# Key and query preparation of a sparse-attention mixer spread over other work, the first norm tile by tile, and banks opened one at a time

## The reference

```python
def rms_norm(x, g):
    return x * rsqrt(mean(x * x, -1) + EPS) * g
def apply_rope_2(x, cos, sin):
    x1, x2 = split(x, 2, axis=-1)
    return concatenate([x1 * cos - x2 * sin, x2 * cos + x1 * sin], -1)

# first block: the norm that starts the kernel, then one projection
hn = rms_norm(h, mix_norm_pre[l]);  proj = hn @ w_in[l]
# each feed-forward layer: up products, gate, down products
y = (silu(a) * b) @ w_out

# third mixer: h is the modulated norm, 4 key heads, 16 query heads of 64
kv = h @ w_kv                                # k_cmp v_cmp k_sel v_sel k_win v_win
kc = rms_norm(silu(blocks(k_cmp) @ w1[0]) @ w2[0], k_norm[0])    # 31 compressed keys
vc = silu(blocks(v_cmp) @ w1[1]) @ w2[1]
ks = apply_rope_2(rms_norm(k_sel, k_norm[1]), cos, sin)
kw = apply_rope_2(rms_norm(k_win, k_norm[2]), cos, sin)
q  = rms_norm(h @ w_q, q_norm)
q_rope = apply_rope_2(q, cos, sin)
s_c = q @ kc * scale        # compressed branch uses q; the two others use q_rope
```

## Time and profile before

| | us |
|---|---|
| median of 3 runs (2306.75 to 2307.64) | 2307.42 |
| the execution that was profiled | 2307.61 |
| its span in the trace | 2305.8 |
| PE busy | 2135.4 (93%) |
| DVE busy | 1261.0 (55%) |
| ACT busy | 808.6 (35%) |
| POOL busy | 91.8 (4%) |

### The profile page before, as it was taken

One profiled execution on the slowest core, in us unless ns is written; L12 is line 12 of the kernel. 1 busy time (PEld: TensorE's weight loads), 2 busy tenths in 40 slices (PEclk: granted clock), 3 DMA queues, 4 the chain that ended last, 5 costly groups with the idle time before them and its releaser, 6 DMA issues.

```text
span 2305.8 us, 28424 instructions
## 1 busy us (share of the span) xinstructions
PE 2135.4 (93%) x10880; PEld 1738.8 (75%) x10880; DVE 1261.0 (55%) x2209; ACT 808.6 (35%) x1467; POOL 91.8 (4%) x88
## 2 busy tenths in 40 slices
PE   4998898999899899999999999999669999999998
PEld 3876576888788688887788877779546667888787
DVE  2578447777654423683755545664566756322234
ACT  3333445333323435213422222333236644222232
POOL 0002300000000010000000000000210110000000
PEclk8999899999999899999999999999779999999999
DMA  4321113556442132101465636323300013422221
GB/s 150 110 73 55 37 56 119 183 183 190 139 162 94 65 95 98 46 1 56 134 204 168 197 117 211 119 64 95 103 1 2 2 38 117 137 94 92 92 92 55
DMA packets 146642, 233.10 MB, mean 101 GB/s; under 512 B 7276, under 2 KB 83532, under 8 KB 146252
## 3 DMA queue, kind: packets, MB, share of 16 engines
q1 hardware_dynamic: 142304, 222.28, 29.9%
q10 hardware_dynamic: 3340, 5.85, 0.7%
q0 software_dynamic: 864, 3.15, 0.4%
HBM read 229.16 MB, written 2.10 MB: 100 GB/s over the span
## 4 chain that ended last, share of the span: by engine, by line
PE 78%; DVE 12%; ACT 4%; issue 4%; POOL 1%; DMA 0%; ACTq 0%; DVEq 0%; POOLq 0%
PE ps L2096 10%; PE ps L2098 10%; PE ps L2097 10%; PE ps L2121 4%; PE ps L2363 4%; PE ps L2122 4%; PE ps L2123 4%; PE ps L2280 4%; PE ps L2056 4%; PE ps L2058 4%; PE ps L2057 4%; PE ps L2282 3%; PE ps L2142 3%; PE ps L2154 2%; PE ps L2167 2%
## 5 line engine op out<-in xcount | busy, mean ns | idle before, releaser
L1512 DVE TENSOR_TENSOR w_lo<-ring,w_hi 128x1024 fp32r<-128x1024 f32 (+4 forms) x362 | 376.5, 1041 | 795.9 <-ACT w_hi L946 795.2
L946 ACT ACTIVATE w_hi<-ring 128x1024 fp32r<-128x1024 f32 (+4 forms) x362 | 329.5, 912 | 992.3 <-PE ps L2098 467.3
L2096 PE MATMUL ps<-x_hi,w_hi 128*128 128x512 f32 x1056 | 415.9, 394 | 0.0
L2098 PE MATMUL ps<-x_hi,w_lo 128*128 128x512 f32 x1056 | 411.2, 389 | 0.0
L2097 PE MATMUL ps<-x_lo,w_hi 128*128 128x512 f32 x1056 | 410.8, 389 | 0.0
L2097 PEld LDWEIGHTS ps<-x_lo,w_hi 128*128 128x128 f32 x1056 | 198.3, 188 | 42.7 <-issue 1.9
L2096 PEld LDWEIGHTS ps<-x_hi,w_hi 128*128 128x128 f32 x1056 | 198.3, 188 | 42.3 <-issue 1.9
L2098 PEld LDWEIGHTS ps<-x_hi,w_lo 128*128 128x128 f32 x1056 | 198.2, 188 | 41.7
L2121 PE MATMUL ps<-w_hi,x_hi 128*128 128x512 f32 x480 | 187.5, 391 | 3.7 <-DVE x_hi L1586 3.7
L2123 PE MATMUL ps<-w_hi,x_hi 128*128 128x512 f32 x480 | 186.8, 389 | 0.0
L2122 PE MATMUL ps<-w_lo,x_hi 128*128 128x512 f32 x480 | 186.8, 389 | 0.0
(11 more groups left out here) (308 smaller groups left out, 3148.8 us busy)
## 6 DMA issues: line engine op xcount, KB each, us to landing
ring<-in_ada_w SPq DMA_DIRECT2D x48, 1024.0 KB, 5.2
ring<-in_ffn_w_in SPq DMA_DIRECT2D x88, 512.0 KB, 4.6
ring<-in_w_up SPq DMA_DIRECT2D x44, 512.0 KB, 4.4
ring<-in_ffn_w_out SPq DMA_DIRECT2D x20, 1024.0 KB, 4.9
ring<-in_hgrn_w_in SPq DMA_DIRECT2D x16, 1024.0 KB, 5.1
ring<-in_w_in SPq DMA_DIRECT2D x12, 1024.0 KB, 5.0
ring<-in_w_down SPq DMA_DIRECT2D x10, 1024.0 KB, 4.9
ring<-in_kv_ada_w SPq DMA_DIRECT2D x8, 1024.0 KB, 5.1
```

What stands on the lines that cost most here:

```text
L946: a.activation(to[:, n % depth, 0:src.shape[-1]], src, ACT.Copy).then_inc(s["hi_done"], 1)
L1512: v.tensor_tensor(to[:, n % depth, 0:width], src, hi[:, n % depth, 0:width].bitcast(F32), ALU.subtract).then_inc(s["lo_done"], 1)
L2096: mm(bs[j], wh[:, k, c], x_hi[:, 2 * q + k], start=first, stop=False)
L2098: ins = mm(bs[j], wl[:, k, c], x_hi[:, 2 * q + k], start=False, stop=last)
```

## The change

**Start.** Only the identity and six row loads stay on ACT's queue. SP loads `x` in four tiles with a semaphore each and waits for nothing, then the unit `iq`, then all other constants (`load_constants`), then the rest of the weights. ACT loads its root table first and takes `x` tile by tile; the rounded parts of the first two weight pieces are made ahead of the norm's output (`EARLY[0]`). The normalized `x` lies where it no longer overlaps `x0_lo`, so DVE splits a bank as soon as it is there. The other rows are transposed into a bank `vec2` between the third and fourth piece of `iq`.

**Feed-forward.** PE opens each of the eight down banks right before its first product. DVE does `ada_out` before `up_gated`.

**Third mixer.** POOL multiplies the norm weights into rotation tables (`rope_g`) once, beside the projections, and is out of the chunks. The key chunks (four of 128x512) are normalized and rotated on DVE between pieces of `nq`. The eight query chunks stand among the products of the compressed keys, by the list `PREP`; the plain form is transposed without the norm weight, which `cmp_norm` now carries. `Q_CHUNKS` and `GROUPS` run from the last token tile to the first.

```diff
+EARLY[0] = [(("iq", q), "iq", q * PIECE, PIECE) for q in range(2)]
+Q_CHUNKS = [(t, j) for t in reversed(range(NT)) for j in range(2)]
+PREP = [("cmp1", 0, 0), ("q", 0), ("cmp1", 0, 1), ("q", 1), ("cmp1", 1, 0), ("q", 2), ("cmp1", 1, 1), ("q", 3), ("cmp2",),
+        ("q", 4), ("q", 5), ("cmpT",), ("q", 6), ("q", 7)]
-XN = {0: xn, ...
+XN = {0: y1, ...
...
 @block.sync
-    sp.wait_ge(s["x_in"], 16)
+    for t in range(NT):
+        sp.dma_start(x_tok[:, t], io["x"][0, t * P:(t + 1) * P, :]).then_inc(s[f"x_in{t}"], 16)
     for n, (pieces, _) in enumerate(units):
+        if n == 1:
+            load_constants()
...
 @block.gpsimd
+    evacuated(pool, ("kvs", 1, NT - 1))
+    pool.wait_ge(s["consts_in"], 32)
+    pool.wait_ge(s["cmp_pos_in"], 64)
+    for j in range(3):
+        gain = qk_norm[:, j, :].rearrange("p (q d) -> p q d", q=2)
+        cos, sin, nsin = [rope_t[:, i] for i in range(3)]
+        for q in range(2):
+            g.tensor_tensor(rope_g[:, j, :, 32 * q:32 * q + 32], cos, gain[:, q:q + 1].broadcast_to(...), ALU.mult)
+        g.tensor_tensor(rope_g[:, j, :, 64:96], nsin, gain[:, 1:2].broadcast_to(...), ALU.mult)
+        g.tensor_tensor(rope_g[:, j, :, 96:128], sin, gain[:, 0:1].broadcast_to(...), ALU.mult)
+    g.tensor_tensor(cmp_norm[:, :], cmp_norm[:, :], qk_norm[:, 0, :], ALU.mult).then_inc(s["tables_done"], 1)
-    for t in range(NT):
-        for j in range(3):
-            pool.wait_ge(s["raw_norm"], i + 1)
-            g.tensor_tensor(w, w, qk_norm[...].broadcast_to(...), ALU.mult).then_inc(s["gained"], 1)
...
 @block.scalar
+    act.dma_start(small[:, 0:P], io["c_small"][:, 0:P]).then_inc(s["ident_in"], 16)
-    act.dma_start(small[:, :], io["c_small"]).then_inc(s["consts_in"], 16)
-    act.dma_start(x_tok[:, :, :], ...).then_inc(s["x_in"], 16)
...
 def norm(i):
     if i == 0:
-        act.wait_ge(s["x_in"], 16)
         for t in range(NT):
+            act.wait_ge(s[f"x_in{t}"], 16)
             x_rms(0, t)
+        early_highs(0, slice(0, 2))
+        evacuated(act, "vec")
...
+    if (key, k) == (("nq", 0), 6):
+        raw_root(NT, slice(16, 24))
...
 @block.vector
-    if i == 0:
-        filled(dve, ("xT", 0, KT - 1))
     for kt in range(KT):
+        if i == 0 and kt in (0, 2):
+            early_lows(0, slice(kt // 2, kt // 2 + 1))
...
-    up_gated(i, FFN_UNITS - 1)
     for u in (FFN_UNITS - 2, FFN_UNITS - 1):
         for mj in ada_after.get((i, u), []):
             ada_out(*mj)
+    up_gated(i, FFN_UNITS - 1)
...
+    if (k, q) == (0, 3):
+        p = filled(dve, "vec2")
+        v.tensor_copy(vec[:, CONV:416], p[:, CONV:416]).then_inc(free("vec2"), 1)
+        step(v.tensor_copy(masks[:, :, :], mask_rows))
...
+def k_chunk(t):
+    a, b = n_a[:, t % 2], n_b[:, t % 2]
+    step(v.tensor_tensor(a, raw[:, t, 16:24, :], <reciprocals>, ALU.mult))
+    dve.wait_ge(s["tables_done"], 13)
+    for j in range(2):
+        rope_gained(a[:, f], t, 1 + j, b[:, f], ko[:, t, f], 4)
+    v.tensor_tensor(ko[:, t], b, ko[:, t], ALU.add).then_inc(s["rope2_done"], 1)
+K_CHUNK_AT = {(("nq", 0), 7): 0, (("nq", 1), 1): 1, (("nq", 1), 7): 2, (("nq", 2), 1): 3}
...
+def q_chunk(i):
+    dve.wait_ge(s["raw_norm"], 2 * i + 2)
+    if i >= 2:
+        filled(dve, ("nT", i - 2, 1))
+    rope_gained(n_a[:, i % 2], t, 0, n_b[:, i % 2], n_o[:, i % 2], 8)
+    if i + 1 < len(Q_CHUNKS):
+        q_norm(i + 1)          # waits for the plain transposes of chunk i - 1
+    v.tensor_tensor(n_o[:, i % 2], n_b[:, i % 2], n_o[:, i % 2], ALU.add).then_inc(s["rope2_done"], 1)
+for i in range(len(Q_CHUNKS)):
+    q_chunk(i)                 # then cmp_sums() after 4, cmp_keys() after 5, cmp_turned() after 6
...
 @block.tensor
-    bs = [open_bank(("down", i, j)) for j in range(8)]
+    bs = [None] * 8
...
+        if k == 0:
+            bs[2 * t + half] = open_bank(("down", i, 2 * t + half))
...
+    if (k, q) == (0, 2):
+        other_rows()
```

More of the change, by code:

```diff
@@ L866, in early_highs @@
                 for key, slot, at, n in EARLY.get(i, [])[some]:
[L867 removed]
+                    high(key, arrived(act, slot, (0,))[:, at:at + n], w2_hi if i in (2, 4) else w_hi if i else w0_hi)
             def post(stage):
@@ L1219, in n_result, with raw_root @@
                 ins.then_inc(free((name, u, k)), 1)
+            def raw_root(done, heads):
+                act.wait_ge(s["raw_done"], done)
+                sums, roots = [stat[:, at:at + 96].rearrange("p (t h) -> p t h", t=NT)[:, :, heads] for at in (32, 128)]
+                a.activation(roots, sums, ACT.Sqrt, scale=1.0 / HD, bias=eps[:, :]).then_inc(s["raw_rms"], 1)
             for g, (key, k) in enumerate(N_PIECES):
@@ L1288, in early_lows @@
                 for key, slot, at, n in EARLY.get(i, [])[some]:
-                    low(key, arrived(dve, slot, (0,))[:, at:at + n], *((w2_lo, w2_hi) if i in (2, 4) else (w_lo, w_hi)))
+                    low(key, arrived(dve, slot, (0,))[:, at:at + n], *((w2_lo, w2_hi) if i in (2, 4) else (w_lo, w_hi) if i else (w0_lo, w0_hi)))
             def norm(i):
@@ new lines, in cmp_sums @@
+            def cmp_sums():
+                p = filled(dve, "cmp2")
+                step(v.tensor_copy(kc_raw, p[0:NCMP, 0:256]))
+                v.memset(kc_t[:, :, :, :], 0.0).then_inc(s["cmp_zero"], 1)
+                dve.wait_ge(s["cmp_zero"], 2)
+                for gg in range(GROUP):
+                    ins = v.tensor_copy(vc_diag[32 * gg:32 * gg + NCMP, :, gg], p[0:NCMP, 256:512].rearrange("p (h d) -> p h d", h=4))
+                    if gg < GROUP - 1:
+                        step(ins)
+                ins.then_inc(free("cmp2"), 1)
+                after()
+                step(v.tensor_tensor(kc_tok, kc_raw.rearrange("p (h d) -> p h d", h=4), kc_raw.rearrange("p (h d) -> p h d", h=4), ALU.mult))
+                after()
+                v.tensor_reduce(stat[0:NCMP, 244:248], kc_tok, AX, ALU.add).then_inc(s["cmp_sq"], 1)
@@ new lines, in cmp_second @@
+            def cmp_second():
+                for kv in range(2):
+                    for j in range(2):
+                        evacuated(pe, ("cmp1", kv, j))
+                pe.wait_ge(s["w2_in"], 32)
+                b = open_bank("cmp2")
+                for kv in range(2):
+                    for kh in range(NSA_KV):
+                        for n in range(2):
+                            ins = mm(b[0:NCMP, kv * 256 + kh * HD:kv * 256 + (kh + 1) * HD], h1[:, kv, n, kh], w2_sb[:, kv, n, :],
+                                     start=(n == 0), stop=(n == 1))
+                ins.then_inc(full("cmp2"), 1)
@@ new lines, in _ @@
+            for what in PREP:
+                if what[0] == "cmp1":
+                    cmp_first(what[1], what[2])
+                elif what[0] == "q":
+                    q_turn(what[1])
+                elif what[0] == "cmp2":
+                    cmp_second()
+                else:
+                    cmp_turn()
+            for t in range(NT):
+                evacuated(pe, ("kT", t))
+            for i in range(len(Q_CHUNKS)):
+                for n in range(2):
+                    evacuated(pe, ("nT", i, n))
```

323 lines of the change are left out of this document (160 added, 163 removed).

## The result

| | before | after |
|---|---|---|
| median of the runs | 2307.09 us (2305.27 to 2307.64, 4 runs) | 2243.6 us (2242.27 to 2244.93, 4 runs) |
| ratio | | 0.9726, 95% interval 0.9709 to 0.9743 |
| profiled execution, span | 2305.8 us | 2240.7 us |
| mean granted clock in it | 0.962 | 0.973 |
| PE, DVE, ACT, POOL busy | | 2124.0, 1257.8, 806.5, 78.9 us |

The account below looks back on a forecast made before the run. PE was taken as the bound (78% of the chain), so gains come only where PE waits: 2307.6 - 22.5 - 18.5 - 26.5 = 2240 us, forecast's own range 2233 to 2247, stated range 2231 to 2257.

Parts of the forecast that it names:

- The start: Part 1, up to the first projection: loading x first and earlier splits gain 22.5 us, ends 18 and 25.
- two banks are enough for the first product: Start: PE's first product needs only two split banks of normed x, so it comes at 18.8 us.
- Rival (c): Start: six row loads still land at 17.8 us, norm ends 8 us later, total 2248; chance 0.07.
- The turns: Part 2, up to down products in three feed-forwards: waits go and clock stays up, 18.5 us, ends 13.1 and 19.
- the 5.3 for the clock in the sum: Turns: no 1.2 GHz stretch behind the three removed waits, gaining 2.0, 1.7 and 1.6 us.
- The third mixer: Part 3, last projection to compressed branch: branch starts 27.2 us earlier, less 0.7, gaining 26.5 us, ends 8 and 32.
- The tables: Third mixer: GpSimd's tables end at 1588.3 or 1590, first key chunk wants them at 1587.4; PE loses 0.7 us.
- The walk through both streams: Third mixer: PE and DVE followed wait by wait behind the projections, last copy at 1664.4 us.
- the surcharge for the clock: Third mixer: 2.4 us added for one quarter at 1.2 GHz and its last transposes, moving the end to 1667.
- Rival (a): Third mixer: clock stays at 1.2 GHz between query blocks, branch at about 1683, total 2256; chance 0.18.
- rival (e): Slower than before: first projections stay at half clock, no gain at the turns, total near 2325; chance 0.02.
- the three lower ends: Smallest gains forecast for start, turns and third mixer: 18, 13.1 and 8 us.

Follow-up runs that it names:

- the bank mended: Changed kernel with first rows' transposes on bank 7 and the norm's tiles on banks 0 to 7, so the first projection's bank is the norm's first tile: 2233.48 us.
- the order with two quarters ahead: Changed kernel with two quarters of the third mixer's compressed-key products, instead of one, ahead of the first query block: 2237.46 us.
- the alternating order alone: Tested by undoing it: changed kernel with all four quarters of the compressed-key products ahead of the first query block: 2243.31 us.
- the fillers: Overwritten identity products ahead of PE's waits at the sixth to eighth query blocks, added to the changed kernel with new bank plan and two quarters first: 2229.72 us.
- the slowest of the filler kernels: The fillers' kernel with more overwritten identity products in the first mixer and ahead of the normed tiles of four norms: 2246.12 us.
- the kernel without fillers: Changed kernel with both the first projection's new bank plan and two quarters of compressed-key products ahead of the first query block: 2230.32 us.

## Why the prediction was right, and where it was wrong

**The start** was to give 22.5 us and gave 16.3 up to the index stage: too much by 6.2. The step that failed is "two banks are enough for the first product". They are enough for its operands. The sentence looked at what the first product reads and not at where it writes, though the plan of banks stood in the code. Its first bank was the one that the norm gives back last, at 25.75. Before the change this cost nothing: the weights came later than all copies. Mending it gave 6.3 us at the first product and 6.8 up to the index stage. The loads were forecast 1 us too early (13.8 against 14.8), and the rest of the sum held: with the bank mended, the first product stands at 19.6 against 18.8. The five row transposes take 0.8 us (1.1 forecast); with the clock behind the first product the stretch up to the index stage lost 0.2. The loads in tiles and the earlier splits weren't undone by themselves, so what each of them gives isn't shown.

Rival (c), the row loads, did not come about: PE's first transpose comes at 9.50. Its argument, that what counts is what stands ahead of a load, fits the run with the constants ahead of the weights, where the DMA engines were busy throughout; what part of the 6.8 us is the 10.0 us of issues stays open.

**The turns** were to give 18.5 us and gave 7.6 + 4.8 + 5.0 = 17.4. No first down product waits, and undoing the opening alone brings back 12.5 us of waits and 3.7 more (6.0 in the profiled executions), near the 13.1 and the 5.3 for the clock in the sum. That DVE's new order for the modulation sum matters only for the eighth tile was right in mechanism: 1.04 us.

**The third mixer** was to give 26.5 us and gave 29.8 (30.2 less 0.4 in the projections). The tables were late by 1.5 us and PE lost 0.71, as taken. The walk through both streams was close: first query pair 10.1 us after the last projection (10.4 forecast), second products done at 28.9 (28.8), sums done at 32.3 (31.8), branch at 43.0 (43.2, before the surcharge for the clock). The step that was mis-sized is what stood beside that surcharge. The quarter at 1.2 GHz came as foreseen (6.20 against 3.73 us). But in the walk a block of eight transposes stood at 1.6 us, from rows at 1.2 GHz, among quarters at 2.4 GHz. At full clock the three blocks between the quarters took 0.9 each: from 1608.49 to 1609.37 is one. The slow quarter cost 2.4 us and these gave 2.1 back, so the walk's end held and the 2.4 us on top of it were too many. That PE's losses do reach the end is shown by the order with two quarters ahead: with that quarter at full clock and the waits of 1.96 and 2.01 down to 0.62, the branch came 5.7 us earlier.

Not all of the 29.8 us is traced to an edit. Putting the key chunks back costs 12.2, and the alternating order alone is worth nothing. DVE's waits for GpSimd, 14.1 us before, are gone, but taking GpSimd out of the chunks wasn't undone by itself.

Rival (a), the clock at 1.2 GHz between the query blocks, did not come about: 1.00 in 1610 to 1620, where quarters and transposes alternate without a pause. The rule of the Trainium skill (TensorE: Matmul & The Clock Gate, Part 4) that transposes don't count as activity did not decide this stretch, since products stood beside them. That the clock is 0.50 again from 1625 to 1635, with transposes in drips, fits the rule and fits an idle engine as well, and the fillers, which kept the clock at 1.00 there, put products in and took the idle time away at once. The first norm does tell the two apart. Up to the first product PE makes nothing but transposes, and here are sixteen of them, first in the kernel with the bank mended, then in the changed kernel:

```profile
15.25 1.91 PE L2112 MATMUL ps<-small,arena 128*128 128x128 f32 x16
```

```profile
15.67 3.62 PE L2111 MATMUL ps<-small,arena 128*128 128x128 f32 x16
```

They take 1.91 us in one and 3.62 in the other, that is 2.4 and 1.2 GHz. So transposes alone raised the clock here, 4 us ahead of the first product at 19.58, which speaks against the rule and for the idle time. The stretch that seemed to agree with it in the prediction was one in which PE stood idle for more than half of the time.

The errors, -6.2, -1.1 and +3.3, cancelled in part: that the total of 2240 was 3.6 us off, with one term off by 6.2, is in part luck.

Two sums of the prediction don't come out. By its own terms rival (e) ends near 2339 and not near 2325 (2307.6 + 65 - 23 - 26.5 + 16). And 2257 doesn't take in all ends of the forecast: the lower end of the third part alone (8 us) gives 2258.6, and the three lower ends together give 2268.5.

## What to carry to other kernels

When a stage is moved earlier, ask for its first instruction not only what it reads but where it writes, and who gives that place back last; a plan of buffers that cost nothing behind a wait of 20 us is the next bound once the wait is gone. Walk a stretch with all durations taken at the same clock, and change that clock for whole stretches. Time saved by a change that moves other stages comes with a change of the clock there, so compare the traces event by event before the total is put down to the edit. Where two engines alternate, place the work so that neither starts the alternation empty, rather than alternate from the first step.

## What was not expected of the hardware

- Seventeen loads of constants and rows (1392 KB) kept SP's queue busy for 10.0 us, 0.59 us each in the mean. Put ahead of the first weights they moved the first product by 6.8 us; the DMA engines were busy all that time (share 1.04).
- Transposes alone can raise the clock: sixteen took 1.91 us ahead of any product in one execution, 3.62 in another.
- A higher mean clock is no gain by itself. It was 0.989 in the slowest of the filler kernels (2246.12 us) and 0.973 in the kernel without fillers (2230.32 us).
- After a wait of 6.9 us, the time that PE spends at 1.2 GHz differs between the profiled executions of two kernels that are alike there: a mean clock of 0.72 or of 0.54 over 30 us. Four executions of one kernel lay 5.7 us apart and in the order of their mean clocks (0.972 to 0.976).
- An identity multiplied by itself in f32 is two instructions of 0.115 us each in these traces, like the 128x124 products of the compressed keys.
